# Moving the two state transposes of a chunked RWKV-7 scan within the TensorE order

## The reference, cut to what matters

```python
def rwkv7_scan(s0, r, decay, k, v, kk, a, reverse):
    def step(s, inp):
        r_t, w_t, k_t, v_t, kk_t, a_t = inp
        sa = jnp.einsum('bhvk,bhk->bhv', s, kk_t)
        s = (s * w_t[:, :, None, :] - sa[..., None] * (kk_t * a_t)[:, :, None, :]
             + v_t[..., None] * k_t[:, :, None, :])
        return s, jnp.einsum('bhvk,bhk->bhv', s, r_t)
```

## Time and profile before

| what | us |
|---|---|
| timed runs: lowest, median, highest of 3 | 1103.64, 1105.39, 1105.43 |
| the profiled execution's own time | 1102.38 |
| its span, first to last instruction | 1100.7 |
| TensorE busy in the span | 1007.3 |
| VectorE busy | 644.0 |
| ScalarE busy | 427.1 |
| GpSimd busy | 406.1 |
| first DMA of the scan to first DMA of the output part | 495.93 to 946.26 |

### The profile page before, as it was taken

The page is one execution under the profiler, slowest core; times in us unless marked ns, Lnnn a source line. Parts: engine busy times, 40 slices in busy tenths (PEclk is TensorE's granted clock), DMA queues, the critical chain, the costliest instruction groups (busy, mean ns, idle before and its releaser), DMA issues. The chain is left out here.

```text
span 1100.7 us, 32049 instructions
## 1 busy us (share of the span) xinstructions
PE 1007.3 (92%) x14407; PEld 907.2 (82%) x14407; DVE 644.0 (59%) x954; ACT 427.1 (39%) x708; POOL 406.1 (37%) x372
## 2 busy tenths in 40 slices
PE   5699999999999999983699989999999997799997
PEld 3299999999989889963699989999899987466685
DVE  5440069585366221343678878888888885356532
ACT  5351201101133343122366655565565652534311
POOL 8111112111206332212556545556666664312200
PEclk9799999999999999995699999999999999989999
DMA  9612422111122110000000000000000000540331
GB/s 355 260 39 82 158 77 78 39 39 39 39 82 82 39 39 1 1 1 10 2 4 4 4 14 4 4 4 4 4 4 4 4 4 4 224 160 26 127 115 58
DMA packets 30036, 61.46 MB, mean 56 GB/s; under 512 B 3352, under 2 KB 21444, under 8 KB 28748
## 3 DMA queue, kind: packets, MB, share of 16 engines
q1 hardware_dynamic: 29900, 59.42, 15.4%
HBM read 49.68 MB, written 9.73 MB: 54 GB/s over the span
## 5 line engine op out<-in xcount | busy, mean ns | idle before, releaser
L681 PE MATMUL ps<-input_rounded,weights_rounded 128*128 128x386 f32 x768 | 263.5, 343 | 4.7 <-DVE input_rest L788 3.3
L683 PE MATMUL ps<-input_rounded,weights_rest 128*128 128x386 f32 x768 | 260.0, 339 | 0.0
L682 PE MATMUL ps<-input_rest,weights_rounded 128*128 128x386 f32 x768 | 259.8, 338 | 0.0
L1412 POOL TENSOR_TENSOR arena<-arena,lvl 128x512 f32<-128x512 f32 x108 | 139.4, 1305 | 76.7 <-ACT arena L1329 46.7
L681 PEld LDWEIGHTS ps<-input_rounded,weights_rounded 128*128 128x128 f32 x768 | 144.7, 188 | 12.1 <-issue 7.5
L470 POOL TENSOR_TENSOR weights_rest<-arena,weights_rounded 128x2048 fp32r<-128x2048 f32 x16 | 75.8, 4740 | 210.7 <-ACT weights_rounded L515 210.7
L682 PEld LDWEIGHTS ps<-input_rest,weights_rounded 128*128 128x128 f32 x768 | 144.8, 189 | 0.5
L683 PEld LDWEIGHTS ps<-input_rounded,weights_rest 128*128 128x128 f32 x768 | 145.0, 189 | 0.0
L1128 PE MATMUL ps<-arena 64*64 64x64 f32 x2880 | 105.4, 223 | 18.0 <-issue 14.7
L1128 PEld LDWEIGHTS ps<-arena 64*64 64x64 f32 x2880 | 93.9, 136 | 23.6 <-issue 17.1
L1138 PE MATMUL ps<-arena 64*64 64x64 f32 x2880 | 105.3, 224 | 5.1 <-DVE arena L1538 4.8
(11 more groups left out here) (247 smaller groups left out, 1705.6 us busy)
## 6 DMA issues: line engine op xcount, KB each, us to landing
arena<-in_w_in SPq DMA_DIRECT2D x16, 1024.0 KB, 5.3
arena<-in_ada_w SPq DMA_DIRECT2D x7, 1024.0 KB, 5.2
mix_scratch<-zc SPq DMA_DIRECT2D x4, 1158.0 KB, 9.6
out<-arena SPq DMA_DIRECT2D x9, 512.0 KB, 3.1
zc<-in_x_sample SPq DMA_DIRECT2D x4, 1024.0 KB, 9.0
hT<-in_ada_w SPq DMA_DIRECT2D x4, 1024.0 KB, 12.0
zc<-in_w_out SPq DMA_DIRECT2D x4, 1024.0 KB, 13.9
arena<-in_x_sample SPq DMA_DIRECT2D x8, 512.0 KB, 3.7
```

The source lines that it names most:

```text
L681: pe.matmul(o, w_hi[:, k, cut], hi_of_h[:, k, cols_b], start=(k == 0), stop=False)
L682: pe.matmul(o, w_hi[:, k, cut], lo_of_h[k][:, cols_b], start=False, stop=False)
L683: last = pe.matmul(o, w_lo[:, k, cut], hi_of_h[:, k, cols_b], start=False, stop=(k == KT - 1))
L1412: pool.tensor_tensor(Um[l % 3], UT, lvl[:, l, :].unsqueeze(1).to_broadcast([P, 2 * PAIRS, C]), ALU.mult).then_inc(q_um[l], 1)
```

## The change

The transpose of the cached state moves behind `lora` of step 0, and TensorE doesn't wait for its copy there: the wait (`q_s0`) moves into `rhs_begin` of chunk 0, the first that writes bank 3 afterwards. ScalarE's copy moves behind `rate(0)` in its step 1.

The transpose of the final state moves from step 6 into step 19, between `update(17, 3)` and `product(17, 4)`, and goes to bank 5, whose last user is the copy of the last keys (`q_kv`). There is no wait for its copy. ScalarE's copy moves to step 19, behind `copy_y(17, 3)`.

```diff
                 def rhs_begin(n):
                     state = S[min(n // PC, 1)]
+                    if n == 0:
+                        pe.wait_ge(q_s0, 1)
...
-                def turn_state(of, done):
+                def turn_state(of, b, done):
...
-                            last = pe.matmul(by_channel(3)[r, d, a, :], of[r, d, a, :], eyes[r, :], start=True, stop=True)
+                            last = pe.matmul(by_channel(b)[r, d, a, :], of[r, d, a, :], eyes[r, :], start=True, stop=True)
...
                 def first_state():
                     pe.wait_ge(q_sl, 64)
-                    turn_state(S[1], q_si)
-                    pe.wait_ge(q_s0, 1)
+                    turn_state(S[1], 3, q_si)
 
                 def final_state():
                     pe.wait_ge(q_st, PC)
-                    pe.wait_ge(q_rh, PC + 3)
-                    turn_state(S[0], q_fs)
-                    pe.wait_ge(q_fc, 1)
+                    pe.wait_ge(q_kv, 2 * N)
+                    turn_state(S[0], 5, q_fs)
 
                 pe.wait_ge(q_init, 1)
-                first_state()
...
                         transpose_keys(n1)
+                    if n2 == N - 1:
+                        final_state()
                     if 0 <= n2 < N:
                         product(n2, 4)
...
                         lora(n0)
+                    if n0 == 0:
+                        first_state()
...
-                    if n2 == PC + 2:
-                        final_state()
                     if 0 <= n2 < N:
                         outputs_begin(n2)
...
                 act.wait_ge(q_init, 1)
-                act.wait_ge(q_si, 1)
-                act.activation(S[1], by_channel(3), ACT.Copy).then_inc(q_s0, 1)
...
-                    if n3 == PC + 2:
-                        act.wait_ge(q_fs, 1)
-                        act.activation(S[0], by_channel(3), ACT.Copy).then_inc(q_fc, 1)
...
                         rate(n1)
+                    if n1 == 0:
+                        act.wait_ge(q_si, 1)
+                        act.activation(S[1], by_channel(3), ACT.Copy).then_inc(q_s0, 1)
...
                         copy_y(n2, 3)
+                    if n2 == N - 1:
+                        act.wait_ge(q_fs, 1)
+                        act.activation(S[0], by_channel(5), ACT.Copy).then_inc(q_fc, 1)
```

## The result

| | kernel before | changed kernel |
|---|---|---|
| median of 4 timed runs, us | 1104.52 (1100.89 to 1105.43) | 1092.61 (1091.66 to 1093.50) |
| the profiled execution's own time | 1102.38 | 1092.30 |
| its span | 1100.7 | 1090.6 |

The ratio is 0.9902, 95% interval 0.9880 to 0.9923. Between the two profiled executions it is 10.1 us.

A forecast was written before the change was run, and what follows sets the result against it. TensorE was taken to bound the kernel inside the scan. Savings of 5.75 us (start) and 3.25 (step 6), less 0.1 at the end, gave 1105.39 - 8.9 = 1096.5 us against the median, range 1093.8 to 1099.2.

The forecast's parts named there:

- The start: Scan start: transpose_v begins at 497.52 instead of 503.27, saving 5.75 us; the moved transpose and copy hide in idle time.
- Rival (b): Scan start: TensorE isn't free at 497.5, so the gain there is only 2.72 us; 1099.5 us in all, chance 0.06.
- Rival (a): Scan start: clock rises within the longer TensorE stretch, lora takes 1.8 us less; 1094.7 us in all, chance 0.07.
- The middle: Step 6: removing the final state's transpose, copy and wait saves 3.25 us, the difference of steps 25.43 and 22.18.
- lower bound of 1.79: Step 6: least gain, the visible time from the transpose at 651.00 to the end of TensorE's wait at 652.79.
- (c): Step 6: the 3.25 us are slack another engine takes, only 1.79 goes; 1098.0 us in all, chance 0.05.
- (d): Scan's early steps: half clock lasts steps longer, at 4.9 us each; 1111.2 us with three more, chance 0.02.
- (e): Whole kernel: the change does nothing, as both holds lie beside a bound elsewhere; 1105.4 us, chance 0.02.
- The end: Step 19: the final state's transpose nearly fits TensorE's hole before product(17, 4), costing 0.1 us, bounds 0 to 0.15.
- The step to the median: From the profiled execution, 3.0 us faster than the timed median, to the median: 1105.39 - 8.9 = 1096.5 us.
- The sum against the profiled execution: Whole kernel: 1102.38 - 5.75 - 3.25 + 0.1 = 1093.5 us, with a span of 1091.8.
- The clock: Scan start: rises and falls of the granted clock may land differently by execution, allowed 1.5 us either way.

The follow-up runs named there:

- after_filled_more: Changed kernel plus matmuls whose result nobody reads in every TensorE hole at the scan's start; 1087.39 us, ratio 0.9865 to the kernel before.
- scalar_hold_only: Changed kernel, but final state transposed in step 6 into bank 5, without TensorE's own wait, ScalarE's copy at its old place; 1095.63 us, ratio 0.9935.
- final_only: Kernel before with only the final state's transpose moved as in the change, the cached state's left ahead of the loop; 1098.72 us, ratio 0.9964.
- before_again: Kernel before, unchanged, run as a second copy for another trace; median 1101.25 us, ratio 0.9982, its profiled execution 1105.52 us.
- turn_one_level_later: Changed kernel with the final state's transpose one level later, between update(17, 4) and product(17, 5), ScalarE's copy behind copy_y(17, 4); 1092.63 us, ratio 0.9904.

## Why the prediction was right and wrong

**The start** was right in each step: no wait for the loads, the transpose and the copy hidden, 5.75 us. That 497.52 came out to the hundredth is luck: the 0.05 us from one engine to the next were drawn from a row that shows 931.46 - 931.36 = 0.10. The measured gap at this place was 0.05. Rival (b), TensorE not ready, is out. Rival (a), the clock rising within the stretch, is out as well: with `transpose_v`, `lora` and the transpose in one stretch the clock stayed at 0.50 until 518.3. Only in `after_filled_more`, where the stretch goes on without a pause past 507.7, did it rise. So the rule of the Trainium skill, "TensorE: Matmul & The Clock Gate", section "Part 1: The HAM clock gate", that activity releases the throttle, agrees with the trace of `after_filled_more` and not with that of the changed kernel, where the stretch from 497.52 to 504.45 ended at 0.50 (the clock rose at 518.3, behind `gram`, which began at 513.68).

**The middle** was right in its size, 3.25 us, and in taking the difference of the steps, not the visible wait. That it has two parts, TensorE's and ScalarE's, was misleading: by `scalar_hold_only` ScalarE's place in the order is enough for all of it. Of the 3.25 us, 0.83 are the matmuls and 2.42 the hold. My lower bound of 1.79 counted TensorE's visible wait as a sure gain; freeing TensorE alone was worth nothing. Rivals (c), (d) and (e) are out.

**The end** failed as a term. I priced 32 matmuls in the hole at +0.1, with bounds of 0 and 0.15, and looked only at what they could delay. They delayed nothing (2.02 us from `update` to `product` in both), and they took away up to 3.2 us that the kernel before loses in the part of its executions in which the clock falls in this hole. A bound below nothing was missing, and for it I had the row: the same engine, waiting 0.79 and 0.86 us between groups of 32, as at the scan's start, where the clock was low. The row was a reason to allow for a fall, not a proof of one: the same waits stand 16 us earlier without it.

**The step to the median** failed with it. I saw that the profiled execution was 3.0 us below the median and carried the difference over unchanged, as if it were a constant. It was the mark of those other executions. The sum against the profiled execution (1093.5) was 1.2 us off; the one against the median 3.9. Set against the kernel before with its hole filled, the sum is right to 0.2 us in one set and to 0.9 in the other. What is left of the 3.9 us, about 1, is the small pieces of the table of stretches. **The clock** term of 1.5 us either way, put only at the start of the scan, was ample there: over the ten traces without filling at the start the stretch from the first `transpose_v` to step 2 takes 47.3 to 48.8 us, 0.75 either way. It was missing at the end.

Still open: what decides in which executions the clock falls in the open hole, why two copies of one kernel had such different shares (12 of 20 and 2 of 12), and why it falls behind the barrier in `final_only`.

## What to carry to other kernels

When timed runs of a kernel lie in two groups some us apart, or a profiled execution lies off the median, look for the stretch in which the two differ before a sum is set against either; more than one trace of the kernel before is worth its price. The mean granted clock of each timed run tells the groups apart without a trace. Independent work that has to be done anyway belongs where the bounding engine has holes, and its price there can be below nothing if it keeps the clock up. And of an engine that waits for a copy look first at what is queued behind that copy on the other engine: here that order alone made the whole 2.4 us, and freeing the visible wait alone gained nothing.

## What the runs showed of the hardware

- TensorE's granted clock fell from full to 0.50 not only in idleness but in work broken by waits of 0.8 us (groups of 32 small matmuls, before_again at 931.3), in some executions and not in others of the same kernel at nearly the same times: `update(17, 3)` began at 929.44 in one and 928.90 in the other. With the gap open it fell there in three traces of six, with 32 matmuls in it in none of six. Two waits of the same lengths 16 us earlier didn't bring it down in either trace.
- 32 matmuls whose result nobody reads, placed in that gap, made the kernel 2.9 us faster in the median (0.9977 of its time); 448 in the holes at the scan's start made the changed kernel 4.5 us faster (1087.39 against 1091.85, in different sets; 4.4 us of it in the traces, 43.54 against 47.97 for the stretch).
- The clock doesn't come back at a fixed time from the first matmul: in `after_filled_more` TensorE had worked without a pause for 10.2 us, from 497.56, when it rose at 507.8; in `turn_one_level_later` it fell at 922.5 and was back at 925.9.
